# Expert stage of a hybrid decoder block: gate and up products computed one after the other, each split over TensorE's column halves

## What is computed

```python
def hier_moe(h, w_group, b_group, w_router, b_router, w_gate, w_up, w_down):
    ...
    for gi in range(N_EXPERT_GROUPS):
        hid = (jax.nn.silu(jnp.einsum('td,edf->tef', ht, w_gate[gi]))
               * jnp.einsum('td,edf->tef', ht, w_up[gi]))
        y = y + jnp.einsum('tef,efd->td', hid * cw[:, gi, :, None], w_down[gi])
```

## Time and profile before

| what | value |
|---|---|
| median of 3 runs | 1557.26 us (1556.84 to 1557.4) |
| the profiled execution, its own time | 1559.59 us |
| span of its trace | 1557.7 us |
| mean granted TensorE clock | 0.995 |
| TensorE busy | 1510.4 us, 97% |
| VectorE busy | 682.2 us, 44% |
| ScalarE busy | 231.6 us, 15% |
| transfers | 589.96 MB, mean 379 GB/s |

### The profile page before, as it was taken

One profiled execution on the slowest core, in us unless ns is written; L12 is line 12 of the kernel. 1 busy time (PEld: TensorE's weight loads), 2 busy tenths in 40 slices (PEclk: granted clock), 3 DMA queues, 4 the chain that ended last, 5 costly groups with the idle time before them and its releaser, 6 DMA issues.

```text
span 1557.7 us, 19266 instructions
## 1 busy us (share of the span) xinstructions
PE 1510.4 (97%) x7980; PEld 811.0 (52%) x7980; DVE 682.2 (44%) x1228; ACT 231.6 (15%) x443; POOL 41.4 (3%) x57
## 2 busy tenths in 40 slices
PE   5999999999999999999999999999999999999996
PEld 2888888855654446444434434434434434434432
DVE  3574767776887636232332332332332322322325
ACT  2100311121322303011010010011010011010003
POOL 1001000000001200000000000000000000000003
PEclk9999999999999999999999999999999999999998
DMA  9999677799878996899999999999999999999993
GB/s 361 397 385 365 259 270 271 280 359 352 305 289 319 364 387 269 364 427 427 428 429 427 429 429 427 429 428 429 398 423 429 428 428 429 428 428 429 427 429 164
DMA packets 102802, 589.96 MB, mean 379 GB/s; under 512 B 6224, under 2 KB 16944, under 8 KB 77408
## 3 DMA queue, kind: packets, MB, share of 16 engines
q1 hardware_dynamic: 100384, 580.93, 91.9%
q0 software_dynamic: 1696, 5.66, 1.1%
q10 hardware_dynamic: 672, 2.66, 0.4%
HBM read 587.07 MB, written 2.16 MB: 378 GB/s over the span
## 4 chain that ended last, share of the span: by engine, by line
PE 66%; DMA 25%; SPq 5%; DVE 2%; issue 1%; ACTq 0%; ACT 0%; DVEq 0%
DMA ring<-in_w_up 22%; PE bank L1165 21%; PE bank L925 7%; PE bank L1198 7%; PE bank L675 5%; SPq L380 5%; PE bank L1079 4%; PE bank L641 4%; PE bank L866 4%; PE bank L1059 3%; PE bank L709 2%; DMA ring<-in_w_ada 2%; PE bank L688 1%; PE bank L691 1%; DMA ring<-in_w_in 1%; PE bank L1090 1%
## 5 line engine op out<-in xcount | busy, mean ns | idle before, releaser
L1165 PE MATMUL bank<-ring,RN 128*64 128x512 f32 x1488 | 330.9, 593 | 9.4 <-DMA ring<-in_w_up 9.4
L1165 PEld LDWEIGHTS bank<-ring,RN 128*64 128x64 f32 x1488 | 106.5, 137 | 223.1 <-issue 199.0
L1198 PE MATMUL bank<-ring,RN 128*64 128x512 f32 x992 | 219.7, 595 | 0.5 <-issue 0.5
L2216 DVE TENSOR_TENSOR RN<-bank,RN 64x512 f32<-64x512 f32 x31 | 21.5, 693 | 376.1 <-ACT RN L1519 376.1
L1198 PEld LDWEIGHTS bank<-ring,RN 128*64 128x64 f32 x992 | 68.9, 137 | 137.4 <-issue 135.6
L2223 DVE COPY RG<-bank 64x512 f32<-64x512 f32 x64 | 44.1, 689 | 196.1 <-PE bank L1198 188.4
L1059 PEld LDWEIGHTS bank<-RN,RX 128*128 128x128 f32 x976 | 111.5, 192 | 13.0 <-issue 13.0
L1059 PE MATMUL bank<-RN,RX 128*128 128x128 f32 x976 | 115.7, 277 | 0.0
L925 PE MATMUL bank<-ring,RT 128*128 128x512 f32 x256 | 113.0, 596 | 0.8 <-DVE RT L2003 0.8
L1165 PE MATMUL bank<-RT,RN 128*64 128x512 f32 x256 | 112.3, 592 | 0.0
L1079 PE MATMUL bank<-RG,RN 128*128 128x512 f32 x240 | 109.5, 599 | 0.0
(11 more groups left out here) (395 smaller groups left out, 1472.6 us busy)
## 6 DMA issues: line engine op xcount, KB each, us to landing
ring<-in_w_down SPq DMA_DIRECT2D x64, 2048.0 KB, 15.5
ring<-in_w_up SPq DMA_DIRECT2D x48, 2048.0 KB, 20.9
ring<-in_w_gate SPq DMA_DIRECT2D x47, 2048.0 KB, 17.3
ring<-in_w_ada SPq DMA_DIRECT2D x32, 2048.0 KB, 10.5
ring<-in_w_in SPq DMA_DIRECT2D x18, 2048.0 KB, 9.2
RT<-in_w_gate SPq DMA_DIRECT2D x17, 2048.0 KB, 15.5
RH<-in_w_up SPq DMA_DIRECT2D x16, 2048.0 KB, 20.0
ring<-in_w_ada SPq DMA_DIRECT2D x48, 512.0 KB, 11.6
```

Of the source, the lines that this page charges most:

```text
L1165: last = mm(bank[0][64 * s:64 * s + 64, :], tokT[:, k, q * CAP:(q + 1) * CAP], w[:, k % 8, :], start=k == 0, stop=k == KT - 1, skip_group_ ...
L1198: last = mm(bank[2 + n % 2][64 * (n // 2):64 * (n // 2) + 64, :], hidT[:, k * CAP:(k + 1) * CAP], wdn[:, n * BLK:(n + 1) * BLK], start=k = ...
```

## The change

Every expert now runs as the last one did, with the pieces in another order. `row_blocks(n, q, w)` computes one piece: piece n (0 and 1 are gate, 2 and 3 are up) of eight row blocks, even ones into rows 0 to 63 and odd ones into rows 64 to 127 of `bank[n // 2]`. The gate's sum of halves is taken by ScalarE (copy) and VectorE (add) after piece 1. Silu is then written twice, to both halves of `sil`, and VectorE multiplies it with up's two halves on 128 rows. `hidden_T` replaces the transposes: four f32 products of `hid`'s blocks with a 128 x 64 matrix `twice` (two identities, one above the other), which transposes and sums the halves together. The result lies contiguously in `bank[0]`, and one ScalarE copy takes it to `hidT`. `expert_halves` hands out the pieces as g0, g1, u0, u1, d0, d1.

```diff
-                return [g[:, 0:4096], u[:, 0:4096], g[:, 4096:8192], u[:, 4096:8192], d[:, 0:4096], d[:, 4096:8192]]
+                return [w[:, c:c + 4096] for w in (g, u, d) for c in (0, 4096)]
...
+            def row_blocks(n, q, w, ks=range(8)):
+
+                for i in ks:
+                    k = 8 * (n % 2) + i
+                    c = CAP * (k % 2)
+                    last = mm(bank[n // 2][c:c + CAP, :], tokT[:, k, q * CAP:(q + 1) * CAP], w[:, i, :],
+                              start=k < 2, stop=k >= KT - 2, skip_group_check=True)
+                if ks[-1] == 7:
+                    last.then_inc(sig("expert_used").sem, 1)
+
+            def hidden_T():
+
+                for f in range(4):
+                    last = mm(bank[0][:, f * CAP:(f + 1) * CAP], hid[:, f:4 * P:4], twice, start=True, stop=True)
+                last.then_inc(sig("hiddenT").sem, 1)
...
+                        w = AHEAD if ahead and n == 2 else ODD[n] if q == 1 and n < 2 else ring[:, n, :, :]
+                        for m in range(2):
+                            if q == 0 and n < 2:
+                                pe.wait_ge(sig("gathered_used").sem, p * 4 + (2 * n + m + 1))
+                            row_blocks(n, q, w, range(4 * m, 4 * m + 4))
+                        if n == 0 and first:
                             gather_part(1, 3)
-                        for s in range(2):
-                            n = 2 * (k // 8) + s
-                            w = AHEAD if ahead and n == 2 else ODD[n] if q == 1 and n < 2 else ring[:, n, :, :]
-                            last = mm(bank[0][64 * s:64 * s + 64, :], tokT[:, k, q * CAP:(q + 1) * CAP],
-                                      w[:, k % 8, :], start=k == 0, stop=k == KT - 1, skip_group_check=True)
-                            if k % 8 == 7:
-                                last.then_inc(sig("expert_used").sem, 1)
...
                     pe.wait_ge(sig("hidden").sem, e + 1)
-                    for f in range(4):
-                        last = tr(bank[1][:, f * P:(f + 1) * P], hid[:, f:4 * P:4], ident)
-                    last.then_inc(sig("hiddenT").sem, 1)
+                    hidden_T()
...
-                    act.wait_ge(sig("expert_used").sem, e * HB + 4)
-                    fn(sil[64:128, :], bank[0][0:64, :], ACT.Silu).then_inc(sig("silu").sem, 1)
+                act.wait_ge(sig("expert_used").sem, e * HB + 2)
+                fn(sil[0:64, :], bank[0][64:128, :], ACT.Copy).then_inc(sig("gate_half").sem, 1)
+                act.wait_ge(sig("gate_sum").sem, e + 1)
+                fn(sil[0:64, :], hid[0:64, :], ACT.Silu)
+                fn(sil[64:128, :], hid[0:64, :], ACT.Silu).then_inc(sig("silu").sem, 1)
...
+                fn(hidT, bank[0][:, 0:4 * CAP], ACT.Copy).then_inc(sig("hiddenT_copied").sem, 1)
...
+                    dve.wait_ge(sig("gate_half").sem, e + 1)
+                    tt_op(hid[0:64, :], bank[0][0:64, :], sil[0:64, :], ALU.add).then_inc(sig("gate_sum").sem, 1)
...
-                        tt_op(hid[0:64, :], bank[0][64:128, :], sil[64:128, :], ALU.mult).then_inc(sig("hidden").sem, 1)
+                    dve.wait_ge(sig("silu").sem, e + 1)
+                    dve.wait_ge(sig("expert_used").sem, e * HB + 4)
+                    tt_op(hid[:, :], bank[1][:, :], sil[:, :], ALU.mult).then_inc(sig("hidden").sem, 1)
...
-            step(v.memset(hid[64:128, :], 0.0))
+            step(tt_op(twice, ident[:, 0:CAP], ident[:, CAP:P], ALU.add))
```

More of the change, by code:

```diff
@@ L293, in block_kernel @@
         hidT = RN[:, 3328:3584]
+        twice = RN[:, 4096:4096 + CAP]
         ohw = RN[:, 3584:3840].rearrange("p (t s) -> p t s", t=TT)
@@ L1085, in last_expert @@
                 for n in range(4):
-                    w = ODD[n] if n < 2 else ring[:, n, :, :]
                     pe.wait_ge(sig(f"odd_landed{n}" if n < 2 else f"expert_landed{n}").sem, 16 * (p + 1 if n < 2 else e if n == 2 else e + 1))
[L1088 to L1091, removed]
-                    last.then_inc(sig("expert_used").sem, 1)
+                    row_blocks(n, 1, ODD[n] if n < 2 else ring[:, n, :, :])
                 pe.wait_ge(sig("ohw").sem, p + 1)
@@ L1138, in pair @@
                     first = isinstance(p, int) and e == 0
[L1139 to L1142, removed]
+                    if ahead:
+                        wait(pe, "over_read")
+                    for n in range(4):
+                        if n == 2 and ahead:
+                            wait(pe, "ahead_landed", 16)
+                        elif n == 2 and not first:
+                            pe.wait_ge(sig("expert_landed2").sem, e * 16)
+                        elif n >= 2:
+                            pe.wait_ge(sig(f"expert_landed{n}").sem, e * 16 + 16)
+                        elif q == 0:
+                            pe.wait_ge(sig(f"expert_landed{n}").sem, p * 16 + 16)
+                        else:
+                            pe.wait_ge(sig(f"odd_landed{n}").sem, p * 16 + 16)
+                        w = AHEAD if ahead and n == 2 else ODD[n] if q == 1 and n < 2 else ring[:, n, :, :]
[4 more added lines that the diff above has]
+                        if n == 0 and first:
@@ L1143, in pair @@
                             gather_part(1, 3)
-                        if k == 12 and first:
+                        if n == 1 and first:
                             wait(pe, "over_counted")
                             inc(mm(bank[7][:, 192:193], ones[:, :], rt[:, 200:201], start=True, stop=True), "over_sum")
-                        if k == 0 and ahead:
-                            wait(pe, "over_read")
-                        if k % 8 == 0:
-                            for s in range(2):
-                                n = 2 * (k // 8) + s
[L1152 to L1161, removed]
@@ L1233, in _ @@
                             for k in range(KT):
-                                last = mm(bank[s][:, :], h2T[:, k, tt * P:(tt + 1) * P], ring[:, 2 * (k // 8) + s, k % 8, :],
+                                last = mm(bank[s][:, :], h2T[:, k, tt * P:(tt + 1) * P], ring[:, 2 * s + k // 8, k % 8, :],
                                           start=k == 0, stop=k == KT - 1)
@@ L1522, in expert_act @@
                     fn(ohwT, bank[7][:, 0:S], ACT.Copy).then_inc(sig("ohwT_copied").sem, 1)
[L1523 to L1530 removed]
+                act.wait_ge(sig("hiddenT").sem, e + 1)
+                fn(hidT, bank[0][:, 0:4 * CAP], ACT.Copy).then_inc(sig("hiddenT_copied").sem, 1)
                 act.wait_ge(sig("expert_used").sem, e * HB + (5 if last else 6))
```

28 lines of the change are left out of this document (removed).

## The result

| what | before | after |
|---|---|---|
| median, us | 1557.3 | 1588.85 (1587.9 to 1590.6) |
| ratio to before, 95% interval | | 1.0201 (1.0189 to 1.0213) |
| the profiled execution, own time | 1559.59 | 1588.17 |
| its span | 1557.7 | 1586.2 |
| TensorE busy | 1510.4 | 1549.1 |

The account below looks back on a forecast made before the run. TensorE (28.54 us an expert) and then weight transfers (29.40) were taken as bounds, waits costing 13.2 us. -13.2 + 14.1 - 0.2 - 0.1 gave +0.6, so 1557.8 us, no change (60 in 100); range 1549.5 to 1566.

Parts of the forecast that it names:

- Hidden blocks: Eight strided loads at 118 ns replace four transposes on TensorE: 0.47 us more an expert, +14.1 us over 30.
- rival A: Hidden blocks' loads: stride adds 66 ns to a plain load, 0.96 us an expert, +15.3 in all, 1572.6 us; 14 in 100.
- the two ends: Expert 0 and the last expert, where no scatter or gather covers the changed steps: -0.2 and -0.1 us.
- Waits for weights: TensorE's waits for weight transfers in 30 experts would go, covered by the transfers' larger lead: -13.2 us.
- Gate and up products: TensorE's 64 gate and up instructions cost the same in the new arrangement: 0.
- Release of buffers: Transfer hole at expert 0 closes, stream 5.2 us earlier; some 2 us lost again at expert 2's down pieces.
- Transfers' lead: Weight stream gains 6.7 us of lead: 5.2 from earlier release, less 2, plus 3.5 from u1's later deadline.
- Rival B: Hidden blocks' eight loads overlap, under 0.6 us; the transfers' gain then counts, 1550 us; 18 in 100.
- ScalarE and VectorE: Added copy, add and second silu, about 2.5 us, hide beside up products; only the ends change, -0.2 and -0.1.

Follow-up runs that it names:

- experiment 3: Two kernels: the changed kernel plus extra products and transposes in the last expert, loading columns at several steps, into an unread bank; 1605.67 and 1600.99 us, one run each.
- experiment 2: Kernel before, with only the transposes of experts 0 to 30 replaced by the four strided products with `twice`; 1588.76 us, ratio 1.0198.
- experiment 1: Changed kernel, with VectorE writing `hid` block by block so that the hidden products load contiguous columns; 1559.96 us, ratio 1.0016.
- second profile of before: Kernel before, unchanged, a single run for a second trace; 1556.87 us, span 1555.0.
- experiment 4: Changed kernel, with up's halves summed before the hidden blocks, the product on 64 rows and the four strided transposes back; 1554.56 us, ratio 0.9982.
- experiment 5: As experiment 4, but the last expert's hidden part as in the kernel before (product on 128 rows, halves summed after the transposes); 1553.47 us, ratio 0.9974.
- experiment 6: As experiment 4, but with the pieces in the old order g0, u0, g1, u1, each still alone; 1554.77 us, ratio 0.9983.

## Why the prediction was wrong

Against the first profile the span grew by 28.5 us: 0.8 before expert 1 (645.72 against 644.90), 26.6 between expert 1 and the last (896.0 against 869.4), 1.1 after that. The rest of the 31.5 us is that the first profile was itself 2.3 us slow, and the scatter of runs.

- **Hidden blocks, the step that failed.** I put eight loads at 118 ns each, 0.94 us, since strided transposes are 118 ns apart, and called that "a read rate for strided columns". It isn't one. In a plain f32 product the same columns take 233 ns, and eight cost 1.7 to 1.8 us. The term was 30 x 0.47 = +14.1 and measured 30 x 1.33 = +39.9. Even my upper bound (179 ns) was too low, since it added to a plain load the 66 ns that a stride adds to a transpose's load (208 against 142). No bound was there for the case that transposes are read in another way than products. Yet the two contiguous loads, 142 and 192 ns, were a sign of this: I used the difference as an argument against rival A instead of as a reason to distrust the whole comparison.
- **Rival A** was right in its place and its sign. Its price of 0.96 us more an expert should have been 1.33. Put into its own sum, -13.2 + 39.9 - 0.3 = +26.4 on a profiled 1559.59 gives 1586.0, against 1588.17 measured. The remaining 2.2 us are the two ends, +1.9 where I took -0.3. The rule of the Trainium skill that I cited, "SBUF — State Buffer" (section "Door 1: The DMA port swizzle", the note on cachelines), was the warning that held: what the table in experiment 3 shows is a price by 16-byte lines. The same page of the Trainium skill asks for at least two hits on a line (section "Specifications (TRN2)"), and the trace agrees: step 2, with two hits on each line, costs 12 ns, step 4, with one, costs 128. That note of the Trainium skill also says that f32 strides up to 4 are free. Here the measurement differs, at 233 ns against 105. The estimate of 107 ns by the Trainium skill, "TensorE: Matmul & The Clock Gate" (section "LDWEIGHTS (loading the stationary operand)"), holds for contiguous loads (105) alone.
- **Waits for weights.** They went, but not for the forecast's reason, so this term came out by luck. TensorE needed 29.87 us an expert, more than the 29.40 of the transfers, and experiment 2 lost its waits in the same way with the old order. The forecast's reason, a lead that covers a TensorE which is still faster than the transfers, is borne out by experiment 1: 28.96 us an expert, a deficit of 0.44 in each of 30 experts, and no wait. The waits were worth 10.4 us in the second profile of before, so I also took 2.8 too many off, and the 2.3 us that I carried to the median as something apart lay in this very term.
- **Gate and up products**, taken as 0: 13.73 us before and after. Right.
- **Release of buffers.** The hole closed as worked out, and the queue stood again where I said, at the down pieces. It stood there for 3.8 us where I took "some 2". In the versions with cheap hidden blocks the same two windows (668 to 676) give 2.1 to 2.9 us (experiments 1, 4 and 5). Right in kind, and nearly so in size.
- **Transfers' lead.** I added 6.7 us. Experiments 4 to 6 show what it is worth with cheap hidden blocks: 2.5 to 3.6 us in the medians, since at the end the stream's own length is the path. In their traces the expert stage also begins 0.6 to 1.4 us later than in the second trace of before. Counted from the first products of expert 0 to the last ones of up, they take 901.8 to 902.3 us instead of 906.6, so 4.4 to 4.9 of the 6.7 us are there. Rival B's 1550 was therefore too low as well.
- **ScalarE and VectorE.** The covers held in the middle. At the two ends I took -0.2 and -0.1. They came to +0.8 and +1.1, since the eight products take 2.08 us where nothing precedes them, not 1.1.
- **The sum again**, with measured terms and the second profile of before (span 1555.0): -10.4 + 39.9 + 0.7 + 1.1 = +31.3, where 31.2 was measured (1586.2).

## What to carry over

Before a stationary operand gets a strided view, ask whether the load is bare: with few moving columns an f32 load that takes every fourth column costs 230 ns instead of 105, with 512 moving columns it costs nothing more. The duration of one kind of instruction (a transpose) is no price for another (a product), even on the same tile, so an unmeasured price needs a bound that allows for a different mechanism. Here two resources were within 3% of each other. An edit that cost the one 1.3 us a round turned most of it into time (40 us less the 10 of waits that went), and one that helped the other gave back only a few us.

## What the runs showed that I had not expected

- **Transposes hardly pay.** A transpose with step 4 comes 120 ns after the one before, against 110 with step 1. An instruction of a product takes 230 to 233 against 105. Why is open. An f32 product also needs two instructions where a transpose needs one, which doubles its cost once more but doesn't explain the spacing.
- **The granted clock fell behind some rows of bare loads.** In the first kernel of experiment 3 it was 1.00 through 5.0 us of products with 64 moving columns (steps 1 to 4), 0.58 over those with step 8 and 0.50 over the transposes behind them. It was back at 0.99 to 1.00 over the products with 512 moving columns. In the second kernel the clock was 1.00 through 3.7 us of transposes and 3.7 us of strided products, 0.84 over the contiguous products behind them, and then 0.50. In experiment 2 it was 0.57 between 640 and 644 us, after 1.44 us of waiting, the hidden blocks of expert 0 and another 0.52 us of waiting. There the next 32 down products took 8.78 us instead of 7.02 to 7.09. In after, at the same place but with 0.87 us of waiting ahead of the blocks, they took 7.09. Whether that difference decides it was not tested. Strided products are not slowed by it: at 0.50 eight of them (L1096 of the second kernel of experiment 3) still took 1.84 us, 230 ns each. The transposes of the first kernel were, 213 instead of 110 to 120.
- **What stays open.** The expert stage begins up to 1.5 us later in some kernels and runs than in others, from causes before it, and in experiment 5 TensorE stands for 1.19 us before the final scatter, where the second trace of the kernel before has 0.27. The profile names no releaser for it. I followed up neither.
